# Value projection in passes of 512 and 256 columns, weights split a group ahead, modulation sums one tile later

## The reference

```python
# both layers of the second block: c and c_ctx are vectors of 1024
shift_x, scale_x, gate_x = jnp.split(silu(c) @ w_mod[i] + b_mod[i], 3, axis=-1)
shift_c, scale_c, gate_c = jnp.split(silu(c_ctx) @ w_mod[i] + b_mod[i], 3, axis=-1)
# layer 0 of the second block, for 1280 tokens
q, k, v, g = jnp.split(h @ w_in, 4, axis=-1)       # v: 1280 x 1024
```

## Time and profile before

| | |
|---|---|
| median of 3 runs | 3553.93 us (3551.34 to 3558.41) |
| the profiled execution, its own time | 3560.28 us |
| its span in the trace | 3558.5 us |
| TensorE busy | 3030.1 us, 85% of the span |
| VectorE busy | 1658.1 us, 47% |
| GpSimd busy | 1040.9 us, 29% |
| ScalarE busy | 916.8 us, 26% |

### The profile page before, as it was taken

One profiled execution on the slowest core, in us unless ns is written; L12 is line 12 of the kernel. 1 busy time (PEld: TensorE's weight loads), 2 busy tenths in 40 slices (PEclk: granted clock), 3 DMA queues, 4 the chain that ended last, 5 costly groups with the idle time before them and its releaser, 6 DMA issues.

```text
span 3558.5 us, 46710 instructions
## 1 busy us (share of the span) xinstructions
PE 3030.1 (85%) x17023; PEld 2605.3 (73%) x17023; DVE 1658.1 (47%) x2421; ACT 916.8 (26%) x1497; POOL 1040.9 (29%) x612
## 2 busy tenths in 40 slices
PE   3799377979999999849998998888887899788896
PEld 2678376857878878737878887878876678777785
DVE  5721433353333333365456307878833540555543
ACT  2110233211100100031000016667711101444421
POOL 1553000245434444414222221323243423000030
PEclk9899677989999999969998999999998999889997
DMA  2533324102111111102326312212010232222201
GB/s 77 176 114 118 94 53 95 35 17 67 59 47 35 59 47 35 35 0 92 124 99 200 124 70 97 83 53 82 16 49 18 101 120 78 61 55 54 66 30 53
DMA packets 222172, 256.78 MB, mean 72 GB/s; under 512 B 9002, under 2 KB 189519, under 8 KB 222047
## 3 DMA queue, kind: packets, MB, share of 16 engines
q1 hardware_dynamic: 206758, 192.56, 18.6%
q10 hardware_dynamic: 15296, 62.72, 4.5%
HBM read 188.34 MB, written 66.91 MB: 72 GB/s over the span
## 4 chain that ended last, share of the span: by engine, by line
PE 41%; DVE 4%; issue 3%; DMA 2%; ACT 2%; POOL 2%; SPq 1%; DVEq 0%; ACTq 0%; POOLq 0%
PE ps L761 7%; PE ps L762 7%; PE ps L763 7%; PE ps L904 4%; PE ps L1190 3%; PE ps L1086 3%; PE ps L1102 3%; DMA b_vt<-zb 2%; PE ps L816 1%; PE ps L817 1%; PE ps L822 1%; PE ps L868 1%; POOL w_parts L600 1%; PE ps L1166 1%; PE ps L1173 1%
## 5 line engine op out<-in xcount | busy, mean ns | idle before, releaser
L761 PE MATMUL ps<-hh,w_parts 128*128 128x512 f32 (+1 forms) x2416 | 938.6, 388 | 94.6 <-POOL hl L621 67.3
L762 PE MATMUL ps<-hl,w_parts 128*128 128x512 f32 (+1 forms) x2416 | 924.8, 383 | 0.0
L763 PE MATMUL ps<-hh,w_parts 128*128 128x512 f32 (+1 forms) x2416 | 923.4, 382 | 0.0
L600 POOL TENSOR_TENSOR w_parts<-w_raw,zero 128x1024 fp32r<-128x1024 f32 x141 | 300.0, 2128 | 1155.5 <-PE ps L763 753.8
L761 PEld LDWEIGHTS ps<-hh,w_parts 128*128 128x128 f32 x2416 | 461.9, 191 | 206.8 <-issue 72.6
L762 PEld LDWEIGHTS ps<-hl,w_parts 128*128 128x128 f32 x2416 | 462.7, 192 | 89.9 <-issue 4.8
L763 PEld LDWEIGHTS ps<-hh,w_parts 128*128 128x128 f32 x2416 | 461.3, 191 | 88.4
L602 POOL TENSOR_TENSOR w_parts<-w_raw,w_parts 128x1024 fp32r<-128x1024 f32 x141 | 338.4, 2400 | 11.1
L1835 DVE SCALAR_TENSOR_TENSOR f_y<-ps,convv,f_y 128x1023 f32<-128x1023 f32 x44 | 56.4, 1283 | 353.3 <-ACT f_y L1434 353.3
L1434 ACT ACTIVATE f_y<-ps,convv 128x1024 f32<-128x1024 f32 x44 | 53.1, 1207 | 634.5 <-PE ps L763 634.5
L1991 DVE TENSOR_SCALAR_CACHE_REDUCE b_s<-ps 128x640 f32<-128x640 f32 (+1 forms) x128 | 101.3, 792 | 241.9 <-PE ps L1173 241.1
(11 more groups left out here) (234 smaller groups left out, 5271.7 us busy)
## 6 DMA issues: line engine op xcount, KB each, us to landing
w_mod_sb<-in_w_mod SPq DMA_DIRECT2D x16, 1536.0 KB, 7.0
w_raw<-in_w_up SPq DMA_DIRECT2D x44, 512.0 KB, 3.9
w_raw<-in_a_w_in SPq DMA_DIRECT2D x32, 512.0 KB, 4.1
d_raw<-in_w_down SPq DMA_DIRECT2D x22, 512.0 KB, 5.3
w_raw<-in_w_in SPq DMA_DIRECT2D x20, 512.0 KB, 4.5
za_parts<-z_hi ACTq DMA_DIRECT2D x16, 640.0 KB, 3.0
za_parts<-z_lo ACTq DMA_DIRECT2D x16, 640.0 KB, 4.1
d_even<-za_parts SPq DMA_DIRECT2D x16, 640.0 KB, 6.4
```

The costliest lines, as they stand in the source:

```text
L600: pool.tensor_tensor(wh[:, s], w_raw[:, s], zero[:].broadcast_to([P, KT * P]), ALU.add).then_inc(w_high[s], 1)
L761: pe.matmul(out_, w_hi, x_hi, start=start, stop=False)
L762: pe.matmul(out_, w_hi, x_lo, start=False, stop=False)
L763: return pe.matmul(out_, w_lo, x_hi, start=False, stop=stop)
```

## The change

For the value projection each row k of a token tile takes one matmul of 512 columns (high activations by both parts of both slots' weights) and one of 256 columns (rest of the activations by the high weights). The two parts' products lie apart in one bank for each token tile, five banks in turn. ScalarE copies the part from the low weights to `z_out` and VectorE adds the other one to it. A second pair of buffers for the weight parts, `v_parts`, serves the odd groups, so that `split_v` of a group may run while the group before it is still in work. VectorE makes five modulation steps after each token tile from the fourth on. The modulation sums of a pair are made later: in "gelu" those of (i - 1, s) after tile (i, s), with the last ones after "forget"; in the value projection those of group i - 1 after the second token tile of group i, with the last ones between the two first tiles of "a_gate". "forget" splits only the 8 columns that it has loaded.

```diff
         ("a_qk", (8, 8), (8, 8), (16, 16)),
-        ("a_v", (4, 4), (4, 4), (4, 4)),
+        ("a_v", (4, 4), (20, 20), (4, 4)),
...
             for s in range(2):
                 sp.wait_ge(mod_summed[s], 4 * 1 + 4 + 1)
+                sp.wait_ge(w_used[s], W0["a_gate"][s] + 1)
             da_load(0, 0)
...
+        def split_v(pool, i, s):
+            parts = v_parts[:, s] if i % 2 else w_parts[:, s, 1:3]
+            first = W0["a_v"][s]
+            pool.wait_ge(w_landed[s], 16 * (first + i + 1))
+            pool.wait_ge(w_used[s], first + max(i, 1))
+            if i == 1:
+                for z in range(2):
+                    pool.wait_ge(stored[z], 16 * Z0["a_v"][z] + 16)
+            pool.tensor_tensor(parts[:, 0], w_raw[:, s], zero[:].broadcast_to([P, KT * P]), ALU.add).then_inc(w_high[s], 1)
+            pool.wait_ge(w_high[s], first + i + 1)
+            pool.tensor_tensor(parts[:, 1], w_raw[:, s], parts[:, 0].bitcast(F32), ALU.subtract).then_inc(w_split[s], 1)
...
+        def project_by_token(pe, name, mod_layer):
+            for i in range(4):
+                parts = v_parts if i % 2 else w_parts[:, :, 1:3]
...
+                for t in range(TOK // P):
+                    n = TOK // P * i + t
+                    if n >= 5:
+                        pe.wait_ge(acc_free[(n - 5) % 2], A0[name][(n - 5) % 2] + (n - 5) // 2 + 1 + 1)
...
+                            last = pe.matmul(got, hh[:, k, tok], parts[:, :, :, wk], start=(k == 0), stop=(k == KT - 1))
+                        if k < KT - 1:
+                            pe.matmul(got[:, :, 0], hl[:, k, tok], parts[:, :, 0, wk], start=False, stop=False)
...
+                    if i and t == 1:
+                        for s in range(2):
+                            mod_sums(pe, mod_layer, i - 1, s)
...
             if norm:
                 project_first(pe, name, segs, norm)
-                if mod_layer is not None:
-                    for s in range(2):
-                        mod_sums(pe, mod_layer, 0, s)
             with pe.Fori(1 if norm or begun else 0, tiles // 2) as i:
                 for s in range(2):
                     project_tile(pe, name, i, s, segs)
                     if mod_layer is not None:
-                        mod_sums(pe, mod_layer, i, s)
+                        mod_sums(pe, mod_layer, i - 1, s)
...
             project_tile(pe, "forget", 0, 0, LATENT_SEGS)
+            for s in range(2):
+                mod_sums(pe, 0, 3, s)
...
+            project_tile(pe, "a_gate", 0, 0, ALL_SEGS)
+            for s in range(2):
+                mod_sums(pe, 1, 3, s)
+            project_tile(pe, "a_gate", 0, 1, ALL_SEGS)
...
+            def keep_tile(i, t):
+                half, at = divmod(t, 5)
+                got = bank(at).rearrange("p (s w n) -> p s w n", s=2, w=2)
+                to = z_out[:, half, at * 2 * P:(at + 1) * 2 * P].rearrange("p (s n) -> p s n", s=2)
+                dve.wait_ge(a_v_rest, 10 * i + (t + 1))
+                dve.tensor_tensor(to, got[:, :, 0], to, ALU.add).then_inc(acc_free[t % 2], 1)
+
+            with dve.Fori(0, 4) as i:
+                steps = list(MOD_STEPS)
+                for t in range(TOK // P):
+                    keep_tile(i, t)
+                    if t >= 3:
+                        for s, k, v in steps[0:5]:
+                            modulate_step(dve, 1, i, s, k, v)
+                        del steps[0:5]
+                for s in range(2):
+                    modulate_keep(dve, 1, i, s)
+            modulate_gains(dve, 1)
```

More of the change, by code:

```diff
@@ L642, in _ @@
             split_tiles(pool, "gelu", 8, "mix", X_COLS)
-            split(pool, W0["forget"], 0, 0)
+            split_forget(pool)
             split_tiles(pool, "qk", 8)
@@ L802, in mod_sums @@
             last.then_inc(mod_summed[s], 1)
-        def project_by_token(pe, name, tiles, mod_layer):
-            with pe.Fori(0, tiles // 2) as i:
+        def project_by_token(pe, name, mod_layer):
+            for s in range(2):
+                pe.wait_ge(acc_free[s], A0[name][s] + 1)
+            for i in range(4):
+                parts = v_parts if i % 2 else w_parts[:, :, 1:3]
                 for s in range(2):
                     pe.wait_ge(w_split[s], i + (W0[name][s] + 1) + 1)
[L809 to L818, removed]
-                                for s in range(2):
[L820 to L823, removed]
@@ L1647, in rotate @@
                         dve.tensor_tensor(z_lo[:, s, 0:w], z_out[:, s, 0:w], z_hi[:, s, 0:w].bitcast(F32), ALU.subtract).then_inc(r_low[s], 1)
[L1649 to L1672, removed]
@@ new lines, in modulate_step @@
+        def modulate_step(dve, layer, i, s, k, v):
+            done = 30 * i + (15 * s + 120 * layer)
+            if k == 0 and v == 0:
+                dve.wait_ge(mod_in[s], 16 * i + 16 * (4 * layer + 1))
+                dve.wait_ge(mod_summed[s], i + 4 * layer + 1)
+            to, w = mod_acc[:, s, v], w_mod_sb[:, s, k]
+            if k == 0:
+                dve.tensor_scalar(to, w, cond[:, k, v:v + 1], None, ALU.mult).then_inc(mod_mult, 1)
+            else:
+                dve.wait_ge(mod_mult, done + (2 * k + v - 1))
+                dve.scalar_tensor_tensor(to, w, cond[:, k, v:v + 1], to, ALU.mult, ALU.add).then_inc(
+                    *((mod_mult, 1) if k < KT - 1 or v == 0 else (mod_done[s], 1)))
@@ new lines, in modulate_keep, with modulate_gains @@
+        def modulate_keep(dve, layer, i, s):
+            t = 2 * MOD_TILES * i + (MOD_TILES * s + 24 * layer)
+            dve.wait_ge(mod_summed[s], i + (4 * layer + 1) + 1)
+            dve.tensor_tensor(mod[:, bass.ds(t, MOD_TILES), :], bank(6 + s)[:, 0:2 * MOD_TILES].rearrange("p (t v) -> p t v", v=2),
+                              vec[:, bass.ds(t + V_BMOD, MOD_TILES)].unsqueeze(2).broadcast_to([P, MOD_TILES, 2]),
+                              ALU.add).then_inc(mod_kept[s], 1)
+        def modulate_gains(dve, layer):
@@ L1884, in _ @@
             rotate(dve, "a_qk", 16, CTX, TOK)
-            keep_modulation(dve, 1)
+            keep_by_token(dve, "a_v")
             dve.wait_ge(lam_step, 3)
```

91 lines of the change are left out of this document (67 added, 24 removed).

## The result

The changed kernel takes **3562.52 us** (median of ten runs, 3555.48 to 3567.51) against 3555.77 for the kernel before (median of ten, 3551.34 to 3560.67). The ratio is 1.0018 with a 95% interval of 1.0010 to 1.0027: slower by 6.75 us, at the edge of what can be told from no change. Forecast were 3576 us, 22 us slower. The direction held, the size did not.

What follows compares the result with a forecast made beforehand. TensorE was taken as most of the chain, so its waits count, mainly for splits held off by VectorE's steps. Layer 0's +28.6 and the value projection's -6.5 put the median of 3553.9 at 3576 us, range 3560 to 3590.

Steps and rivals of the forecast that it cites:

- The step that failed: Layer 0, "gelu": pair 3's split waits until VectorE's unbroken run ends, so tile (3, 0) starts 21.5 us later, at 208.2.
- The first rival: Splits wait for one step only: layer 0 loses 11 us, value projection stays at -6.5, total 3558; chance 0.08.
- "qk": Layer 0, after "forget": the split for this projection is held until pair 3's steps end, adding 5.4 us.
- The slow clock of 1.7: Layer 0: after the pause before tile (3, 0) TensorE works at its lower clock level for a while, losing 1.7 us.
- Layer 0 together: Layer 0's late sums: 21.5 + 1.7 + 5.4 = 28.6 us slower, bounds 10 and 32.
- Value projection: Layer 1: splits ahead and wider passes start the gate projection at 2014.2 in place of 2024.54, a gain of 10.3 us.
- the ring of VectorE: Value projection: sums, tiles, steps, additions and a split holding VectorE off set each group's pace, 34.6 or 36.6 us.
- TensorE's waits before the sums: Value projection: TensorE waits for `mod_done` after each group's second token tile, about 4 us each time.
- The way in for a split at the next addition: Gate's split, end of value projection: gets the port at VectorE's next addition, a microsecond later, and takes 4.3 us.
- Gate projection: Loses 2.8 us for the last sums between its first two tiles and about 1 us for weights behind a `da_load`.
- the second rival: Steps and splits don't hinder each other where additions lie between: layer 0 loses 9.4, value projection gains 20, 3543 us; chance 0.07.

Runs made afterwards that it cites:

- e10: The changed kernel with one more VectorE wait, before the second slot's first step, for the first slot's last step: 3565.3 us, 1.0025.
- e17: The changed kernel with one VectorE wait for its direct predecessor in the middle of the second slot's steps: 3562.08 us, 1.0023.
- e11: The changed kernel with every modulation step waiting for the one directly ahead: 3584.4 us, 1.0087.
- e1: The changed kernel with layer 0's sums back in their old places, value projection as changed: 3546.26 us, 0.9971.
- e2: The kernel before with only layer 0's sums made late, value projection untouched: 3571.16 us, 1.0039.
- e7: The changed kernel with layer 1's modulation steps from k = 1 on over 48 of 384 columns: 3547.71 us, 0.9982.
- the second look at after: The changed kernel, unchanged, profiled once more: 3561.19 us in all.
- e12: e9 with the one added VectorE wait of e10: 3527.54 us, 0.9925.
- e13: e12 with layer 0's last sums behind the first tile of "qk": 3521.21 us, 0.9904.
- e9: The changed kernel with weights loaded ahead of modulation in "gelu" and value projection, layer 1's last sums ahead of the gate's first tile: 3525.15 us, 0.9912.
- e4: The changed kernel with SP loading weight pairs ahead of the modulation loads in "gelu" only: 3535.79 us, 0.9934.

## Why the prediction was wrong in size

- **The step that failed** is "a waiting split doesn't get in while steps follow each other without a gap". Its term, tile (3, 0) at 208.2 and 21.5 us later, measured 8.05 (194.77). A split is shut out only by a run in which VectorE has not waited for some time; here VectorE had waited until 187.41, and the split got in 2.7 us later, where the held ones asked 8.9 and 10.3 us after its last wait (122.63 against 113.78, 231.96 against 221.67). e10 and e17 show it from both sides, e11 in the first slot. The rows of 134.73 to 137.31 in the kernel before could have warned of it. The first rival had this outcome for this one place (195.3 for the end of the split, +8.6 us), and its total of 3558 lies nearer to 3562.5 than the forecast of 3576. That is in part luck: by its reason the splits of 122.63 and 231.96 too would have been let in after one step, and they were held. This is also where the rule of the Trainium skill (SBUF — State Buffer, "Who interferes with whom"), that each side holds the port for one instruction, agrees with the trace at 190.13 (1.89 us) and not at 122.63 (9.12 us).
- **"qk"**: the split held until the end of pair 3's run was right. Forecast +5.4; from the end of "forget" to "qk" TensorE took 4.53 us before and 242.21 - 231.96 = 10.25 after, which is +5.7. The slow clock of 1.7 measured 1.0 (9.0 us at the end of "forget", less 8.05). Layer 0 together: 8.05 + 1.0 + 5.7 = 14.8, and 15.8 with the 1.0 us by which this execution was ahead at the first step. e1 and e2 say 14 to 16 on medians. Forecast 28.6.
- **Value projection**: right in size and in what bounds it. Group 1 started 32.5 us in (forecast 33.4), the gate projection 145.4 (145.7); steps beside a split took 8.13 us for five, and the ring of VectorE was the bound (e7). TensorE's waits before the sums were shorter than the forecast 4 us (0.82, 2.51 and 1.93). The way in for a split at the next addition is seen at 2020.87 (2.71 us: held for 0.8, until the addition of 2021.75), but the split of 1903.68 (2.35 us) was let in after one step, ahead of the next addition.
- **Gate projection**: +2.8 for the sums and +1.0 for the weights behind `da_load` were forecast. The stretch to its end lengthened from 115.6 to 123.8 us, by 8.2. Of that 2.8 are the sums and 3.32 the wait for weights, issued at 2047.84 and landed at 2058.01. The remaining 2.1 are slow clock: 0.07 x 28.75 + 0.30 x 9.55 = 4.9 us lost after, against 0.18 x 15.46 = 2.8 before. That term was mis-sized by 4.4. The wait itself differs between executions of one kernel: 2.15 us in the second look at after.
- **The sum**: between the two profiled executions it is +12.5 us at the start of the value projection (2.2 less than the 14.8 at "qk"; why is open), -10.6 and +8.2, which gives the +10.1 at the load of `w_all`; then -9.7 in the differential attention and +2.8 behind it, which gives the 3.3 us between the spans. The medians differ by 6.75. The differential attention stood in no term, and since one execution differs from another there by 4.7 us, the sum can't be closed more closely than that. So it also stays open why the change without the late sums wins 10 us (e1), where its two stretches give -10.6 + 8.2 = -2.4 and the differential attention some -5.
- **A reading that was wrong**: the second rival took the 2.98 us of the two `tensor_scalar` steps at 162.68 as a sign that they got through beside a split. Two such steps take 0.75 us when no split is at work, so they were held until the split of 162.71 (2.40 us) was over, and the row speaks against that rival.

## What to carry to other kernels

Where two engines share a port, ask not only whether their instructions collide but how long the one has been running without a wait when the other asks. A wait placed inside a run lets the other in, but the work stays serial: here it won nothing (e10, e17 and e12). Whether it pays where the engine that was shut out is the one on the path is not shown: e13 has such a wait and is 3.9 us faster than e9, but it also moves the last sums, and the move alone was not run. Before moving a consumer later, follow what its release lets SyncE issue: here the late sums were a loss with the modulation loads first in the queue and a gain of 28 us with the weight loads first.

## What was not expected of the hardware

- A run of VectorE steps with two SBUF inputs let GpSimd in at 2.7 us after VectorE's last wait (190.13, 1.89 us) and kept it out at 8.9 us and later (9.12, 7.69 and, in e4, 10.69 us, each to the end of the run). Between lies a border that no run places, and no run tells apart the time since the wait from the number of steps since it. Runs broken by additions that read PSUM, as in the value projection, are another case (2020.87, 2.71 us, though VectorE had last waited 13.6 us before). The cause is argued, not shown: steps that are issued ahead of the engine may leave no gap, and a wait makes one.
- Once GpSimd was in, four split operations went nearly back to back (1.89, 2.53, 2.20, 2.59 us), and VectorE got about one step in between each two. So from then on the two took turns by the instruction, where a held split got no turn until the run was over.
- A step that waits for the one directly ahead costs 0.12 us more (9.12 against 7.49 us for fourteen).
